# Both attentions of a two-layer encoder: a negated maximum in one operation, the softmax division moved behind the product with V, and negated sinks

## The reference, cut to what matters

```python
# layer 0
p = jax.nn.softmax(logits, axis=-1)
attn = p[0] - lam * p[1]
outs.append(jnp.einsum('bhqk,bkhe->bqhe', attn.astype(v.dtype), v[:, :L]))
...
o = rms_norm(o, subln_gain) * (1.0 - lam_init)
# layer 1
m = jnp.maximum(jnp.max(logits, axis=-1, keepdims=True), sink)
p = jnp.exp(logits - m)
p = p / (jnp.sum(p, axis=-1, keepdims=True) + jnp.exp(sink - m))
o = jnp.einsum('bchgqj,bcjhe->bcqhge', p.astype(v_band.dtype), v_band)
```

## Time and profile before

| | us |
|---|---|
| median of 3 runs | 1642.12 (1639.43 to 1643.93) |
| the profiled execution, whole | 1636.11 |
| its span, first to last instruction | 1633.8 |
| attention A, first bias to last product | 140.84 to 181.45 |
| attention B, first logits to last product | 532.00 to 582.95 |
| granted TensorE clock, mean of the span | 0.941 of full |

### The profile page before, as it was taken

The page is one execution under the profiler, slowest core; times in us unless marked ns, Lnnn a source line. Parts: engine busy times, 40 slices in busy tenths (PEclk is TensorE's granted clock), DMA queues, the critical chain, the costliest instruction groups (busy, mean ns, idle before and its releaser), DMA issues.

```text
span 1633.8 us, 22399 instructions
## 1 busy us (share of the span) xinstructions
PE 1492.6 (91%) x6536; PEld 1195.7 (73%) x6536; DVE 1306.2 (80%) x1443; ACT 991.2 (61%) x1300; POOL 98.8 (6%) x149
## 2 busy tenths in 40 slices
PE   6795779999976897899999999999999999999994
PEld 2583557777745685788888888888888888888883
DVE  5897648787664735689999998989989899899984
ACT  3345524334433732578787777778778687777872
POOL 3111111111010000000000000000000000000001
PEclk9996689999997579899999999999999999999997
DMA  9987148998554015699999999999999999999992
GB/s 344 398 319 251 43 138 302 316 345 302 202 219 167 1 52 206 228 378 371 385 385 364 394 383 364 397 379 368 395 380 370 391 377 372 382 376 371 393 375 92
DMA packets 216976, 501.39 MB, mean 307 GB/s; under 512 B 18449, under 2 KB 43233, under 8 KB 216929
## 3 DMA queue, kind: packets, MB, share of 16 engines
q1 hardware_dynamic: 192370, 425.04, 70.6%
q0 software_dynamic: 19760, 71.89, 12.0%
q10 hardware_dynamic: 4800, 3.90, 0.7%
HBM read 487.13 MB, written 13.63 MB: 306 GB/s over the span
## 4 chain that ended last, share of the span: by engine, by line
PE 82%; DVE 10%; DMA 3%; issue 2%; ACT 2%; ACTq 1%; POOL 0%; POOLq 0%; DVEq 0%
PE PS L1330 78%; DVE MOD L915 2%; DVE WLO L903 2%; PE PS L1671 1%; DMA SHR<-in_ada_w 1%; DVE HT_LO L956 1%; PE PS L1398 1%; DVE sm L993 1%; DMA SHR<-toep_rows 1%; DVE ss L965 1%; ACT WHI L576 1%; ACTq L706 0%; PE PS L1360 0%; DVE Q L974 0%; ACTq L707 0%
## 5 line engine op out<-in xcount | busy, mean ns | idle before, releaser
L903 DVE TENSOR_TENSOR WLO<-WRAW,WHI 128x1024 fp32r<-128x1024 f32 x790 | 915.4, 1218 | 94.0 <-ACT WHI L576 94.0
L576 ACT ACTIVATE WHI<-WRAW 128x1024 fp32r<-128x1024 f32 x790 | 778.3, 1053 | 80.7 <-PE PS L1330 73.2
L1330 PE MATMUL PS<-WHI,HT_HI 128*128 128x512 f32 x1280 | 512.6, 401 | 30.6 <-DVE WLO L903 21.7
L1330 PE MATMUL PS<-WLO,HT_HI 128*128 128x512 f32 x1280 | 503.6, 393 | 0.0
L1330 PE MATMUL PS<-WHI,HT_LO 128*128 128x512 f32 x1280 | 430.5, 393 | 0.0
L1330 PEld LDWEIGHTS PS<-WHI,HT_HI 128*128 128x128 f32 x1280 | 243.8, 190 | 83.6 <-issue 19.3
L1330 PEld LDWEIGHTS PS<-WHI,HT_LO 128*128 128x128 f32 x1280 | 243.0, 190 | 52.7
L1330 PEld LDWEIGHTS PS<-WLO,HT_HI 128*128 128x128 f32 x1280 | 244.0, 191 | 48.6
L1330 PE MATMUL PS<-WHI,AT_HI 128*128 128x512 f32 x536 | 214.9, 401 | 6.0 <-DVE WLO L903 6.0
L1330 PE MATMUL PS<-WLO,AT_HI 128*128 128x512 f32 x536 | 209.8, 391 | 0.0
L1330 PE MATMUL PS<-WHI,AT_LO 128*128 128x512 f32 x536 | 209.7, 391 | 0.0
(11 more groups left out here) (184 smaller groups left out, 881.9 us busy)
## 6 DMA issues: line engine op xcount, KB each, us to landing
WRAW<-in_moe_w_in SPq DMA_DIRECT2D x448, 512.0 KB, 6.3
WRAW<-in_moe_w_out SPq DMA_DIRECT2D x224, 512.0 KB, 5.5
SHR<-in_ada_w POOLq DMA_DIRECT2D x80, 512.0 KB, 6.6
WRAW<-in_ffn_w_in SPq DMA_DIRECT2D x88, 256.0 KB, 6.8
WRAW<-in_a_w_qkv SPq DMA_DIRECT2D x24, 512.0 KB, 11.4
WRAW<-in_ffn_w_out SPq DMA_DIRECT2D x22, 512.0 KB, 6.0
SHR<-in_kv_ada_w POOLq DMA_DIRECT2D x16, 512.0 KB, 6.3
WRAW<-in_ada_w SPq DMA_DIRECT2D x16, 512.0 KB, 5.5
```

Source lines behind the costliest of these rows:

```text
L576: nc.scalar.activation(WHI[:, u.split(k), :], WRAW[:, u.raw(k), :], ACT.Copy).then_inc(w_hi, 1)
L903: V_.tensor_tensor(WLO[:, u.split(k), :], WRAW[:, u.raw(k), :], f32(WHI[:, u.split(k), :]), ALU.subtract).then_inc(w_lo, 1)
L1330: return nc.tensor.matmul(out, a, b, start=start, stop=stop)
```

## The change

The negated maximum comes straight from the reduction (`negate=True`), in A into the column that ScalarE reads. In B the sinks are negated once, near the start, so that the minimum of the two negated values takes the place of maximum and negation; the exponential of the sink gets `scale=-1.0`. In A, map 0 is no longer scaled: map 1 is scaled by (1/sum1)(-lambda)(sum0), and `copy_o` on ScalarE multiplies by 1/sum0. In B, the maps are no longer scaled; the transposes wait for the exponentials alone, and VectorE scales the output while it copies it from PSUM (`scaled_o`), two steps later in its own list; ScalarE's `copy_o` goes.

```diff
@@ ScalarE
-                                                 bias=c[:, 2 + m:3 + m])
+                                                 bias=c[:, 2 + m:3 + m], scale=-1.0)
...
-                    nc.scalar.activation(Q[:, i, h * P:(h + 1) * P], PS[:, 6 + n % 2, 0:P], ACT.Copy
-                                         ).then_inc(sems["o_ready"], 1)
+                    nc.scalar.activation(Q[:, i, h * P:(h + 1) * P], PS[:, 6 + n % 2, 0:P], ACT.Copy,
+                                         scale=sm[:, n % S_BUFS, 8:9]).then_inc(sems["o_ready"], 1)
...
-                    if n:
+                    if n and a == "A":
                         copy_o(n - 1)
                 load_table(ACT.Sqrt)
-                copy_o(n_all - 1)
+                if a == "A":
+                    copy_o(n_all - 1)
@@ VectorE
-                    chain(V_.tensor_reduce(mx, buf[:, :, 0:span], axis=AX, op=ALU.max))
-                    if a == "B":
-                        chain(V_.tensor_tensor(mx, mx, sinks[:, 2 * h:2 * h + 2], ALU.max))
-                    V_.tensor_scalar(nm, mx, -1.0, None, ALU.mult).then_inc(sems["negmax"], 1)
+                    if a == "A":
+                        V_.tensor_reduce(nm, buf[:, :, 0:span], axis=AX, op=ALU.max, negate=True
+                                         ).then_inc(sems["negmax"], 1)
+                    else:
+                        chain(V_.tensor_reduce(mx, buf[:, :, 0:span], axis=AX, op=ALU.max, negate=True))
+                        V_.tensor_tensor(nm, mx, sinks[:, 2 * h:2 * h + 2], ALU.min).then_inc(sems["negmax"], 1)
...
                         chain(V_.reciprocal(r, total))
-                        chain(V_.tensor_tensor(r[:, 1:2], r[:, 1:2], neglam[:, 2:3], ALU.mult))
-                        chain(V_.tensor_scalar(s0, s0, r[:, 0:1], None, ALU.mult))
+                        chain(V_.scalar_tensor_tensor(r[:, 1:2], r[:, 1:2], neglam[:, 2:3], total[:, 0:1],
+                                                      ALU.mult, ALU.mult))
                         V_.scalar_tensor_tensor(s0, s1, r[:, 1:2], s0, ALU.mult, ALU.add
                                                 ).then_inc(sems["probs"], 1)
                     else:
                         chain(V_.tensor_tensor(r, total, sm[:, n % S_BUFS, 6:8], ALU.add))
                         chain(V_.reciprocal(r, r))
-                        V_.tensor_tensor(buf[:, :, 0:span], buf[:, :, 0:span], bc(r, span), ALU.mult
-                                         ).then_inc(sems["probs"], 1)
+
+                def scaled_o(n):
+                    i, h = n // HEADS, n % HEADS
+                    dve.wait_ge(sems["pv"], n + 1)
+                    V_.tensor_tensor(Q[:, i, h * P:(h + 1) * P].rearrange("p (m d) -> p m d", m=2),
+                                     PS[:, 6 + n % 2, 0:P].rearrange("p (m d) -> p m d", m=2),
+                                     bc(sm[:, n % S_BUFS, 8:10], 64), ALU.mult).then_inc(sems["o_ready"], 1)
...
-                    probs(n)
+                    totals(n)
+                    if a == "B" and n >= 2:
+                        scaled_o(n - 2)
+                if a == "B":
+                    scaled_o(n_all - 2)
+                    scaled_o(n_all - 1)
...
+            chain(V_.tensor_scalar(sinks[:, :], sinks[:, :], -1.0, None, ALU.mult))
@@ TensorE
-                    pe.wait_ge(sems["probs"], n + 1)
+                    if a == "A":
+                        pe.wait_ge(sems["probs"], n + 1)
+                    else:
+                        pe.wait_ge(sems["expd"], 2 * n + 2)
```

More of the change, by code:

```diff
@@ L992, in biased, with totals @@
                     mx, nm = sm[:, n % S_BUFS, 0:2], sm[:, n % S_BUFS, 2:4]
-                    chain(V_.tensor_reduce(mx, buf[:, :, 0:span], axis=AX, op=ALU.max))
-                    if a == "B":
-                        chain(V_.tensor_tensor(mx, mx, sinks[:, 2 * h:2 * h + 2], ALU.max))
-                    V_.tensor_scalar(nm, mx, -1.0, None, ALU.mult).then_inc(sems["negmax"], 1)
-                def probs(n):
+                    if a == "A":
[4 more added lines that the diff above has]
+                        V_.tensor_tensor(nm, mx, sinks[:, 2 * h:2 * h + 2], ALU.min).then_inc(sems["negmax"], 1)
+                def totals(n):
                     span = (n // HEADS + 1) * P
```

## The result

The changed kernel takes 1627.64 us (median of 4 runs, 1621.00 to 1628.11), the kernel before 1641.48 on the same chip (4 runs, 1639.43 to 1643.93): ratio 0.9906, interval 0.9877 to 0.9935, which is 15.4 us less by the ratio. Run again later, it took 1628.47 (6 runs, 1615.41 to 1630.37) against 1639.62 (11 runs), ratio 0.9927 [0.9904, 0.9951], 12.0 less. The forecast was 7.8 less. The sign was right; the size was short by a third to a half, and 1627.64 lies just under the low end of 1628.5.

A forecast was written before the change was run, and what follows sets the result against it. VectorE was taken to bound A at span 128, both VectorE and TensorE to be full at 256, TensorE to bound B nearly everywhere. 5.1 (A) + 2.8 (B) - 0.1 (sinks) = 7.8 us off 1642.1: 1634.3, range 1628.5 to 1640.

The forecast's parts named there:

- rival d: In A, the negated reduction takes 0.17 us longer: 1635.7 us; its chance was counted within the forecast's 0.55.
- B's start: Start of B: transposes released earlier, T(2) at 539.64 against 541.33, a gain of 1.7 us.
- VectorE's new wait: In B, VectorE stands until products(n-2) end, before scaled_o; claimed to cost nothing.
- TensorE issues logits right after products(n-2): In B, logits(n+3) directly follow products(n-2), taking 0.8 us at span 128, more than scaled_o's 0.29 + 0.04.
- rival c: In B, VectorE, TensorE and ScalarE close into a ring through scaled_o: slower, 1645.5 us; chance 0.05.
- T(6) to T(8): In A, starts of the transposes of heads 6 to 8, forecast at 154.49, 156.53 and 158.88 us.
- worth 0.6 us (bounds 0 and the rival below): In A, the longer run without gaps brings a moment of raised clock earlier or longer: 0.6 us.
- 4.6 by steps: In A, last product at 176.89 instead of 181.45 us, with TensorE at its lower clock throughout: 4.6 us.
- rival (a): Clock goes up in A's second half: A gives 8.6, all 11.4, time 1630.7 us; chance 0.15.
- 1.7 + 1.1: In B, 1.7 us from the earlier start plus 1.1 from TensorE's other three waits going: 2.8 us.
- Rival (b): Saving given back after the attentions, both projections staying at low clock 4.3 us longer: 3.9 lost, 1638.2 us; chance 0.25.
- the DMA share is down to 0.00 in A: In both attentions DMA share is 0.00 and 0.01, a reason the gain should survive to the end.

The follow-up runs named there:

- e6: Changed kernel plus one unused 384-column matmul ahead of each of B's 16 products: 1620.50 us, ratio 0.9869 to the kernel before.
- e7: Changed kernel, but in B TensorE waits for its own last products before the next logits: 1634.17 us, ratio 0.9949 to the kernel before.
- e1: A's part of the change alone, B as in the kernel before: 1633.85 us against 1642.28, ratio 0.9952.
- e4: Changed kernel, but B's transposes wait for VectorE's reciprocals instead of the exponentials: 1626.48 us, ratio 0.9899 to the kernel before.
- e5: Kernel before plus one unused 384-column matmul ahead of each of B's 16 products: 1634.09 us, ratio 0.9974.
- v11: Changed kernel with unused matmuls ahead of B's products, 56 in the wait before B, 9 in B's first gaps: 1614.86 us against 1640.18, ratio 0.9851.
- e3: Kernel before with only the maxima negated in one operation in both attentions, sinks negated once: 1637.29 us, ratio 0.9976.
- e8: Kernel before plus one unused 384-column matmul ahead of each of A's 16 products: 1643.41 us, ratio 1.0014.
- v10: Changed kernel with unused matmuls ahead of A's and B's products, in the waits ahead of both, and behind A: 1621.69 us, ratio 0.9887.

## Why the prediction was wrong in size

**What held.** The steps. VectorE's step of 1.50 (1.49), the reduction at 0.42 and 0.69 (rival d falls), L1010 at 0.22, scaled_o at 0.29, B's start 1.68 (1.7) earlier, and TensorE without a wait in B from 531.6 to the rise of the clock at 551. VectorE's new wait is there, 3.2 us in sum on L1345, and costs nothing: in B's timeline above, logits(5) (532.62) follow products(0) with no wait, as "TensorE issues logits right after products(n-2)" had it. The ring of rival c did not close. Up to the rise of the clock A went by its list too: the transposes of head 4 start 9.61 us behind the first L989 (149.77 - 140.16), forecast 9.39 (150.23 - 140.84), those of head 9 at 20.51 (160.67), forecast 20.31. At the instruction that is not waited for, the step gained what the earlier trace rows had shown: the reciprocal again starts before the reduction ends (0.34 behind its start, for a reduction of 0.42). The sentence of the Trainium skill that the prediction set against this (VectorE: DVE Perf Modes, "The DRAIN you can't avoid") is only half of that section: it also says that a next operation which is not held starts earlier. With that half this trace agrees.

Two small slips in the working move nothing: behind an instruction that is waited for, the next starts 0.03 to 0.04 after its end by the earlier trace rows and not 0.02 to 0.03, and the terms of T(6) to T(8) add up to some 0.1 less than the times given for them.

**The step that failed in A** is "worth 0.6 us (bounds 0 and the rival below)". The mechanism was named: the run without gaps brings the clock up earlier. It came 22 us in instead of as a moment near the end. A gave 7.8 where 4.6 by steps less 0.1 for copy_o was the rest of the sum, so this term measured some 3.3 and not 0.6. The trace puts the place: transposes(9) start 20.51 us behind the first bias where they had started at 24.70 (165.54 in the kernel before), 4.2 less at 0.50 (4.4 forecast), and the other 3.7 come behind the rise, where 0.2 was forecast without the term. Each of the nine profiles with the whole of A's change (blocks of 32.5 to 34.1) has the clock up by 24 us in, and A then goes by VectorE's 2.17 a head. In seven it stays up to A's end; in e6 and e7 it falls back for some us, and theirs are the two longest blocks. When it comes up is not the code's alone: with the same A it was 13 us in (e7) to 24 (e1, e4). All this is rival (a) as it was put, priced at 8.6; 7.8 and, in e1, 7.4 were measured. I gave it 0.15 because B had been full for 20 us at 0.50, and took that as the rule for A.

**The step that failed in B** is the same sentence turned round: in pricing B I took 0.50 as given to its end and counted only waits, 1.7 + 1.1. The earlier trace rows show a stretch of the kernel before that is full and slow, and I took from it that a full stream does not raise the clock there. The windows ahead of it, which I did not weigh, are busy for 7.00 and 9.88 of 10 us; the changed stream has 8.98 and 10.00 in its first two and no wait from 531.6 to the rise. Three edits of the stream alone moved the clock: e5 adds work and B gets 6.2 us shorter; e7 adds waits and B gets 11.5 longer; v11 fills the gaps and B runs at 1.00 throughout. So of the 12.4 us in the profiled execution 2.8 are steps at 0.50, as forecast and as e4 shows up to its transposes(14), and some 9.6, what is left, are the clock in B's last 13 us.

What in the stream the clock follows stays open. The matmuls added in e5, e6 and v11 both close gaps and raise the amount of work, and no run here parts the two; "the streams have lost their gaps" is not enough by itself, since e4's had none for 20 us at 0.50.

The Trainium skill's rule (TensorE: Matmul & The Clock Gate, "What's actually happening": the gate is the default, activity opens it) was named with rival (a), and I set it aside because B of before spoke against it. The direction of that rule is what e5, e7 and v11 show. How soon activity opens the gate no run here fixes.

**The rest of the sum.** In the usual run, at 1628, the change brings 12 us. With A's 7.8 (the nine profiles have 6.5 to 8.1) that leaves about 4 for B, an estimate; e3 and e4 were profiled with such a late rise in B (47.98 and 45.62, that is 3.0 and 5.3 less). No execution of the changed kernel itself of that group was profiled, so where its clock rises is not shown. Nor is what decides between the groups.

**Rival (b)**, the saving given back, can't be told from the spread. Against the profile of before, the stretch from A to B is 2.2 us longer and the rest 3.5; but over the other profiles these two lie at 350.0 to 354.5 and 1050.2 to 1056.3, and that of before (350.55 and 1050.85) is at the low end of both, which goes with its time of 6 us below the median shown. e1 is the other end: its A is 7.4 shorter, and its profiled execution, with 354.46 and 1055.1, takes 1638.51, no less than that of before. An example of what moves there is the first stretch of the experts, 120 matmuls each, before and after:

```profile
642.87:666.00 23.13, 22.19 (x120) 19.56 (x120) 8.44 (x22) 4.91 (x6) 1.67 (x2) 0.86 0.22 73
```

```profile
624.88:650.00 25.12, 24.76 (x120) 21.97 (x120) 7.94 (x19) 4.33 (x5) 1.09 (x2) 0.77 0.21 64
```

The clock (0.86 against 0.77) makes the 2 us of difference; in the second profile of the changed kernel that stretch was short again, and in e1 to e4 it was long. So the gain of 15.2 in the span is 20.2 in the blocks and 0.7 in an earlier start, less 5.7 that any single execution can add or spare.

**A reason of mine that was wrong**, without effect on the sum, is that the DMA share is down to 0.00 in A. The first 10 us of A before read 1.05, the next 10 still 0.29; only the second half is at 0.01 or less:

```profile
140.84:150.84 10.00, 6.12 (x28) 4.01 (x28) 9.09 (x35) 6.41 (x29) 5.47 (x8) 0.50 1.05 400
```

## What to carry to other kernels

Where a stage bound by TensorE shows a granted clock of 0.50, its time is open by up to a factor of 1.8 (1.23 to 0.70 for the same logits; 50.95 to 33.87, or 1.5, for the whole of B, 2.8 us of it by the change's steps), and an edit that removes a wait has two prices: the wait, and the chance that the clock comes up. Price both, and don't take the clock of before as a constant of the stage. When such a stage stays slow, try unused matmuls in it, and in the waits of TensorE ahead of it and in its first steps. Here 81 of them took the gain from 12 to 15 us to 24.4, and the four runs agree within 2 us; with 16 of them alone, in B's steps, it was 21.5 (e6). In the kernel before the same 16 helped in six runs of ten (e5), so repeat the runs. It pays only where TensorE is the bound (e8, and A in v10).

## What the runs showed of the hardware

- A full row of records is no sign of a clock about to rise: 20.00 of 20 us busy at 0.50 in e4; in the changed kernel the clock came up in the middle of such a stretch, 22 us into A and 25 into B. Once up it stayed up to A's end through 1.35 busy of 2 us, the last row here:

```profile
160.00:162.00 2.00, 2.00 (x10) 1.27 (x8) 1.72 (x4) 1.35 (x5) 0.00 (x0) 0.50 0.00 0
164.00:166.00 2.00, 1.35 (x10) 0.92 (x10) 1.89 (x6) 1.71 (x6) 0.00 (x0) 1.00 0.00 0
```

  That is no rule either. In e6, with the same code in A, the clock went back to 0.50 after two windows much like it:

```profile
166.48:168.48 2.00, 1.35 (x11) 0.83 (x11) 1.93 (x5) 1.68 (x7) 0.00 (x0) 1.00 0.00 0
168.48:170.48 2.00, 0.71 (x6) 0.53 (x5) 1.82 (x8) 1.81 (x6) 0.00 (x0) 0.85 0.04 8
170.48:172.48 2.00, 2.00 (x11) 2.00 (x10) 1.24 (x4) 1.09 (x3) 0.00 (x0) 0.50 0.00 0
```

- A kernel can have two times, here 1615 to 1621 and 1627 to 1630, and the mean granted clock goes with them (0.947 to 0.950, 0.938 to 0.940). That the time of the rise in a stage makes the two is likely and not shown. Both profiles fell in the first group, seven of ten runs in the second; a profile alone would have overstated the change.
- A reduction with its result negated costs what a plain one costs (420 and 686 ns). A column as the scale of ScalarE's copy from PSUM adds 0.09 us (366 against 277 ns for 128 columns).
